# The opening of a two-layer encoder: order of the first norm, first weight tiles and one later weight tile

## The reference, cut to what matters

```
h = rmsnorm(x) ; proj = h @ w_in                       (25 column tiles of 128 in the kernel)
x = x + [gated linear attention ; hyena group] @ w_out
x = x + (silu(rmsnorm(x) @ w_gate) * (rmsnorm(x) @ w_up)) @ w_down
log_gate = log_sigmoid(z @ w + b) / 16                 (decay of the attention)
hid = sin(freq1 * (feats @ w1 + b1)) ; hid = sin(freq2 * (hid @ w2 + b2))   (filters of the hyena group)
```

## Time and profile before

| | us |
|---|---|
| median of 3 runs | 1250.37 |
| the profiled execution, whole | 1251.39 |
| its span, first to last instruction | 1249.6 |
| PE busy in the span | 1229.5 (98%) |
| POOL busy | 767.0 (61%) |
| ACT busy | 728.9 (58%) |
| DVE busy | 725.5 (58%) |

### The profile page before, as it was taken

One profiled execution on the slowest core, in us unless ns is written; L12 is line 12 of the kernel. 1 busy time (PEld: TensorE's weight loads), 2 busy tenths in 40 slices (PEclk: granted clock), 3 DMA queues, 4 the chain that ended last, 5 costly groups with the idle time before them and its releaser, 6 DMA issues.

```text
span 1249.6 us, 21579 instructions
## 1 busy us (share of the span) xinstructions
PE 1229.5 (98%) x8224; PEld 1023.3 (82%) x8224; DVE 725.5 (58%) x1068; ACT 728.9 (58%) x1343; POOL 767.0 (61%) x622
## 2 busy tenths in 40 slices
PE   8999999999999999999999999999999999999997
PEld 7767787879988888888877777788898888888886
DVE  6846576677777777300058465664867777760003
ACT  6766665448577767433256766554576777763233
POOL 3656652557488667866626666328365666777662
PEclk9999999999999999999999999999999999999999
DMA  6211112241322222332322212214122223323222
GB/s 241 78 52 52 69 52 69 75 184 51 102 102 102 101 102 84 119 101 101 101 68 68 69 52 69 68 53 145 58 85 102 101 102 108 119 79 135 90 96 84
DMA packets 31496, 115.31 MB, mean 92 GB/s; under 512 B 3489, under 2 KB 4001, under 8 KB 31010
## 3 DMA queue, kind: packets, MB, share of 16 engines
q1 hardware_dynamic: 31394, 113.93, 26.5%
HBM read 111.82 MB, written 2.10 MB: 91 GB/s over the span
## 4 chain that ended last, share of the span: by engine, by line
PE 86%; DVE 6%; ACT 4%; issue 2%; POOL 1%; DMA 0%; POOLq 0%; ACTq 0%; DVEq 0%
PE ps L2151 19%; PE ps L2158 10%; PE ps L1991 6%; PE ps L2011 6%; PE ps L2013 6%; PE ps L2010 6%; PE ps L1993 6%; PE ps L1992 6%; PE ps L2317 2%; PE ps L2303 2%; PE ps L2007 2%; PE ps L2002 2%; PE ps L2004 2%; POOL w_lo L1251 1%; PE ps L2177 1%
## 5 line engine op out<-in xcount | busy, mean ns | idle before, releaser
L1251 POOL TENSOR_TENSOR w_lo<-w_raw,w_hi 128x1024 fp32r<-128x1024 f32 x108 | 265.3, 2458 | 274.0 <-ACT w_hi L713 217.1
L713 ACT ACTIVATE w_hi<-w_raw 128x1024 fp32r<-128x1024 f32 x108 | 114.1, 1056 | 175.5 <-PE ps L2013 157.5
L2151 PE MATMUL ps<-h_parts,w_hi 128*128 128x512 f32 x576 | 204.9, 398 | 0.0
L2158 PE MATMUL ps<-h_parts,w_lo 128*128 128x256 f32 x672 | 189.0, 281 | 0.0
L1991 PE MATMUL ps<-h_parts,w_hi 128*128 128x512 f32 (+1 forms) x392 | 166.3, 424 | 1.7 <-POOL w_lo L1251 0.9
L2151 PE MATMUL ps<-sum_parts,w_hi 128*128 128x512 f32 x432 | 156.3, 402 | 0.0
L1993 PE MATMUL ps<-h_parts,w_lo 128*128 128x512 f32 (+1 forms) x392 | 152.1, 388 | 0.0
L1992 PE MATMUL ps<-h_parts,w_hi 128*128 128x512 f32 (+1 forms) x392 | 151.4, 386 | 0.0
L2158 PE MATMUL ps<-sum_parts,w_lo 128*128 128x256 f32 x528 | 148.6, 281 | 0.0
L1430 DVE TENSOR_TENSOR x<-x,ps 128x512 f32<-128x512 f32 x32 | 20.5, 683 | 210.4 <-PE ps L2007 208.8
L1256 POOL TENSOR_TENSOR w_lo<-w_raw,w_hi 128x512 fp32r<-128x512 f32 x60 | 77.7, 1296 | 87.8 <-ACT w_hi L699 87.8
(11 more groups left out here) (298 smaller groups left out, 2829.3 us busy)
## 6 DMA issues: line engine op xcount, KB each, us to landing
w_raw<-in_units SPq DMA_DIRECT2D x110, 512.0 KB, 3.2
u<-in_pairs SPq DMA_DIRECT2D x44, 512.0 KB, 4.0
w_raw<-in_pairs SPq DMA_DIRECT2D x40, 512.0 KB, 4.0
x<-in_x SPq DMA_DIRECT2D x4, 512.0 KB, 6.8
gain<-in_gain SPq DMA_DIRECT2D x4, 512.0 KB
spec<-in_pairs SPq DMA_DIRECT2D x4, 512.0 KB, 4.9
out_y<-x SPq DMA_DIRECT2D x3, 512.0 KB, 2.6
par<-in_par SPq DMA_DIRECT2D x1, 1214.5 KB, 7.8
```

The lines of the kernel that those rows point to most:

```text
L713: nc.scalar.activation(w_tile(g, 0), w_raw[:, g % RAW], ACT.Copy).then_inc(s_hi, 1)
L1251: nc.gpsimd.tensor_tensor(w_tile(g, 1), w_raw[:, g % RAW], w_tile(g, 0).bitcast(F32), ALU.subtract).then_inc(s_lo, 1)
L2151: nc.tensor.matmul(both(m, p).rearrange("p (v t) -> p v t", v=2), hi[:, cols], factor[m][:, :, k], start=start and k == 0, stop=False, ski ...
L2158: last = nc.tensor.matmul(both(m, p)[:, FIRST] if p >= WIDE else out, lo[:, cols], factor[m][:, 0, k], start=False, stop=k == KT // 2 - 1, ...
```

## The change

It has these parts, all in the opening and the first slots of layer 0:

1. The first norm's squares: one instruction of 1024 columns for each tile in place of two of 512; the root takes its small constant from a memory cell that POOL sets at the start, and DVE's four `x_mean` of the first norm go.
2. ACT's order: unit 0 is rounded ahead of tile 0's tokens, and unit 1 after tile 3's tokens and no more ahead of them.
3. PE's order: transpositions of tiles 2 and 3 both stand between the halves of unit 0, five identity products (in bank 1) behind them, and `net_one` stands behind the second half. The identity products at the start are 2, 4 and 4 in place of 8, 2 and 8.
4. ACT rounds unit 4 of layer 0 between the Exp and the Ln of `gate_logs`, and no more at the head of slot 2.
5. SP issues the transform constants behind unit 2 and no more ahead of it.

```diff
+LOGS_UNIT = 4
@@ SyncE
-            sp.dma_start(cst[:, K_DFT:N_CST], cst_d[:, K_DFT:N_CST]).then_inc(s_dft, 16)
...
                     if L or n >= RAW:
                         load_unit(L * UNITS + n)
+                    if L == 0 and n == RAW:
+                        sp.dma_start(cst[:, K_DFT:N_CST], cst_d[:, K_DFT:N_CST]).then_inc(s_dft, 16)
@@ ScalarE
+            def first_square(tt):
+                act.wait_ge(s_x[tt], 16)
+                nc.scalar.activation(g12[:, D_MODEL * tt:D_MODEL * tt + D_MODEL], x[:, tt], ACT.Square,
+                                     accum_out=ss[:, 2 * tt:2 * tt + 1]).then_inc(xsq.sem, 2)
+
+            def first_root(tt):
+                act.wait_ge(xsq.sem, xsq.at(0, 2 * tt + 2))
+                nc.scalar.activation(rs[:, tt:tt + 1], ss[:, 2 * tt:2 * tt + 1], ACT.Sqrt,
+                                     bias=rs[:, TT:TT + 1], scale=1.0 / D_MODEL).then_inc(xrt.sem, 1)
...
                 for tt in range(2):
-                    x_square(0, tt)
-                    x_root(0, tt)
+                    first_square(tt)
+                    first_root(tt)
+                hi_unit(0)
                 x_round(0, 0)
-                hi_unit(0)
                 x_round(0, 1)
                 for tt in range(2, TT):
-                    x_square(0, tt)
-                    x_root(0, tt)
+                    first_square(tt)
+                    first_root(tt)
                 x_round(0, 2)
+                x_round(0, 3)
                 hi_unit(1)
-                x_round(0, 3)
...
                     nc.scalar.activation(zlog[:, h], zlog[:, h], ACT.Exp, scale=-1.0).then_inc(acs.sem, 1)
+                if L == 0:
+                    hi_unit(LOGS_UNIT)
                 for h in range(HEADS):
...
-                    hi_unit(L * UNITS + slot + 2)
+                    if L * UNITS + slot + 2 != LOGS_UNIT:
+                        hi_unit(L * UNITS + slot + 2)
@@ GpSimd
+            nc.gpsimd.memset(rs[:, TT:TT + 1], EPS)
@@ VectorE, norm_start
                 for tt in range(2):
-                    x_mean(0, tt)
                     x_scale(0, tt)
...
                 for tt in range(2, TT):
-                    x_mean(0, tt)
                     x_scale(0, tt)
@@ TensorE
-            def first_unit(b, g, bank, n, amid=None):
+            def first_unit(b, g, bank, n):
...
-                    if k == KT // 2 and amid is not None:
-                        x_turn(b, amid)
...
-            keep_warm(8)
+            keep_warm(2)
             x_turn(0, 0)
-            keep_warm(2)
+            keep_warm(4)
             x_turn(0, 1)
-            keep_warm(8)
+            keep_warm(4)
...
-                        first_unit(2 * L, g, 0, 0, None if L else 2)
+                        first_unit(2 * L, g, 0, 0)
+                        if L == 0:
+                            x_turn(0, 2)
                         x_turn(2 * L, TT - 1)
                         if L == 0:
-
-                            pe.wait_ge(xlo.sem, xlo.at(0, 5))
+                            keep_warm(5, 1)
+                        first_unit(2 * L, g, 0, 1).then_inc(s_unit, 1)
+                        if L == 0:
                             net_one(0)
-                        first_unit(2 * L, g, 0, 1).then_inc(s_unit, 1)
```

More of the change, by code:

```diff
@@ L713, in hi_unit @@
                 nc.scalar.activation(w_tile(g, 0), w_raw[:, g % RAW], ACT.Copy).then_inc(s_hi, 1)
+            def first_square(tt):
[6 more added lines that the diff above has]
+                                     bias=rs[:, TT:TT + 1], scale=1.0 / D_MODEL).then_inc(xrt.sem, 1)
             def x_square(b, tt):
                 for n in range(2):
[L718 to L723, removed]
+                    act.wait_ge(xres.sem, xres.at(b - 1, 2 * tt + n + 1))
+                    junk = ps[:, norm_banks(b)[tt][n], :]
                     nc.scalar.activation(junk, x[:, tt, half(n)], ACT.Square,
@@ L727, in x_root @@
             def x_root(b, tt):
-                act.wait_ge(xpre.sem, xpre.at(b, tt + 1))
+                act.wait_ge(xpre.sem, xpre.at(b - 1, tt + 1))
                 act.wait_ge(xsq.sem, xsq.at(b, 2 * tt + 2))
@@ L2038, in x_turn, with keep_warm @@
                         t.then_inc(s_unit, 1)
-            def keep_warm(n):
+            def keep_warm(n, bank=6):
                 for _ in range(n):
-                    nc.tensor.matmul(ps[:, 6, 0:P], ident, ident, start=True, stop=True)
+                    nc.tensor.matmul(ps[:, bank, 0:P], ident, ident, start=True, stop=True)
             def net_one(L):
```

## The result

| | before | changed |
|---|---|---|
| median of 7 runs, us | 1251.18 (1250.21 to 1251.88) | 1254.76 (1252.83 to 1255.31) |
| profiled execution, whole, us | 1251.39 | 1253.59 |
| its span, us | 1249.6 | 1251.8 |

The ratio is 1.0027, 95% interval 1.0017 to 1.0037. The forecast was 1250.8, 0.4 over the kernel before, with a range to 1253.0; measured is 3.6 over it, so the time lies outside the range. I had given a slowdown of over 0.2% a chance of 0.13.

A forecast was written before the change was run, and what follows sets the result against it. PE was taken as the bound, busy 1229.5 of 1249.6 us, with PE's and DVE's lines tied at unit 4. The opening's 1.75 us gain was lost to a POOL collision, unit 4 0.4 later: 1250.37 + 0.4 = 1250.8, range 1248.8 to 1253.0.

The forecast's parts named there:

- The opening: Layer 0's start: unit 0 at 13.1 us, 2.6 earlier, unit 1 at 22.8, 1.75 earlier, first sine at 28.2.
- Is a tensor_scalar held?: DVE's first reduce_turn: L1675 taken as held by POOL's rest of unit 2, ending at 24.95 us; 0.29 us alone.
- Rival C: Both reduce_turn chains: tensor_scalar isn't held by POOL, so the kernel takes 1250.1 us; chance 0.17.
- The 0.2 us by which the first clamp gets in: First reduce_turn: L1685 starts at 26.7 us, 0.2 before POOL takes up unit 3's rest at 26.91.
- Rival A: First reduce_turn: L1685 slips behind POOL's rest of unit 3; unit 4 at 45.3 us, total 1252.1; chance 0.17.
- The collision of part 4, and unit 4: POOL's rest at 35.4 us holds DVE's second reduce_turn once; L1685 at 39.7, unit 4 at 43.98, 0.4 later.
- So the start of unit 4 moves the end by as much.: From unit 4 on PE runs nearly without waits, so a 0.4 us later start was carried to the end.
- The 1.75 us of the opening stand in front of unit 4 as PE idle time.: Ahead of unit 4: the opening's 1.75 us gain becomes PE waiting, since DVE's chain is late.
- Rival B: Opening: PE's clock rises only during unit 0, putting unit 4 at 45.9 us, total 1252.8; chance 0.12.
- Rival D: Second reduce_turn: DVE and POOL lose little to each other; unit 4 1.7 us early, total 1248.7; chance 0.08.

The follow-up runs named there:

- part 4 alone: The kernel before with only the rounding of unit 4 moved between Exp and Ln: 1255.0 us, ratio 1.0037 (1.0025 to 1.005).

## Why the prediction was wrong, step by step

- *The opening.* Right to 0.1 us for PE: unit 0 at 13.21 (13.1), unit 1 at 22.84 (22.8). Unit 2 was rounded at 20.44 (20.4) and the sine started at 27.90 (28.2).
- *Is a tensor_scalar held?* Open in the trace before, taken as held. Right: 1.14 and 2.49 us against 0.29. Rival C falls. The trace agrees with the section of the Trainium skill, SBUF — State Buffer, that I had cited ("Who interferes with whom").
- *The 0.2 us by which the first clamp gets in.* Right (26.48 against 26.67). Rival A didn't occur in any profile of the changed kernel or of an experiment with its opening and part 5; the clamp got in by 0.09 us in one of these eight and by 1.15 in another. My sum had an error as large as the margin, so luck has a part in this. POOL's start and ACT's table load both follow unit 3's landing, so a late landing moves them together: in four of the ten experiments' profiles it was 0.6 to 1 us later (unit 4 then starts at 44.3 to 44.7). That alone can't catch the clamp; a late unit 2 can, as the profile with part 4 alone shows.
- *The collision of part 4, and unit 4.* Right in place and size: held once, clamp at 39.43 (39.7), unit 4 0.2 to 0.1 late (0.4).
- *"So the start of unit 4 moves the end by as much."* This is the step that failed, and the sum's two missing terms lie in it. I had asked of POOL's rest of unit 4 only what it meets at its new place, and not what moves into its old one. With that place empty, POOL makes the first exponents 0.7 us earlier and the rest of unit 5 starts 1.1 us earlier, ahead of the running sums: 2.0 us on DVE, 1.9 on PE. The trace before had all of it: the sums at 43.45, which take 0.7 each when alone, and POOL's chain behind its row at 40.66, shown with the result. With POOL's rest kept behind the first sums instead, ACT's order unchanged, the time is 4.5 us lower than the changed kernel's.
- *"The 1.75 us of the opening stand in front of unit 4 as PE idle time."* I priced the wait at its length. It is 2.1 us, and behind it, or behind the second one, PE runs 3.41 us at a granted clock of 0.50, which costs 1.7; the sum had put this term at nothing without a reason. Rival B had the clock in the wrong place: in the opening it rose at 9.45 us in one profile and at 11.63 in the other, against 11.65 before, with fewer identity products. The section on transpositions by which B was likely (the Trainium skill, TensorE: Matmul & The Clock Gate, "Part 4: PE-mode transpose") would have had the rise come late, and it didn't. That doesn't settle the rule: identity products and the gain's products stand among the transpositions, and no run was made for it alone. Nor was the stretch before the rise "half transpositions" in the trace before, as I wrote: from 6.10 to 11.65 us they are 1.9 us of 5.5.
- *Rival D.* The opening's gain does pass, as soon as POOL's rest is off DVE's chain: without part 4 unit 4 starts 2.1 us earlier than before, and the median is 1249.42 against 1250.94.

Open is why the clock falls in some executions and not in others with the same waits: the profile with part 4 alone has waits of 1.6 and 1.9 us and no fall.

## What to carry to other kernels

When work is moved to an idle place of an engine, follow both ends: what it meets where it lands, and what closes up behind it at the place that it leaves; two engines that hold each other must be laid out together. Slack that a faster stage builds up ahead of a bound was not free on TensorE: in four of the five profiles with a PE wait of over 1.5 us in this stretch, 1.7 us more were lost to the lower clock behind it. An experiment that removes one of two causes of the same effect may show nothing; remove both before calling the effect absent.

## What the runs showed of the hardware that I had not expected

- A cast of 128 x 160 from fp32 to bytes took 2.18 us beside POOL's subtraction and 0.23 alone, as much held as the arithmetic.
- In the four profiles with a lower clock behind a wait, PE was 95 to 100% busy during it, and the granted clock was 0.50, the lower of 1.2 and 2.4 GHz.
- The load of unit 3, 512 KB issued at 21.9 to 22.4 us, landed 3.1 to 3.4 us after its issue in eight of the twelve profiles and 4.2 to 4.3 in the other four. No run shows why.
